# Causal latent attention on pairs of heads, and the order of divisions and maxima in the dilated attention

## What is computed

```python
# latent branch: 8 heads, queries and keys of 64 + 32 features, values of 64, fully causal
s = (einsum('nqhe,nkhe->nhqk', qn_b, k_nope) + einsum('nqhr,nkr->nhqk', qp_b, kpe)) * scale
p, _ = masked_softmax(s, kpos[None, :] <= qpos[:, None])
o = einsum('nhqk,nkhe->nqhe', p, v)
# dilated branch: 8 heads of 64, patterns (window, dilation) = (128, 1), (512, 4), (2048, 16),
# each a banded softmax over strided keys; results combined by their softmax denominators
```

## Time and profile before

| | us |
|---|---|
| median of three runs (lowest, highest) | 2237.77 (2235.47, 2243.18) |
| the profiled execution's own time | 2240.37 |
| its span in the trace | 2238.7 |
| latent prompt attention, from its first to its last work | 555.3 to 736.6 |
| latent sample attention | 736.9 to 875.4 |
| dilated prompt attention, transposes of queries and keys included | 875.7 to 1024.5 |
| PE busy (share of the span) | 2136.0 (95%) |

### The profile page before, as it was taken

How to read it: one execution, slowest core, us unless ns; L and a number is a source line. 1 busy time by engine, 2 the same in 40 slices (tenths; PEclk the granted TensorE clock), 3 DMA queues, 4 the chain that set the end, 5 groups by cost and what they waited for, 6 DMA issues and landing times. The chain is left out here.

```text
span 2238.7 us, 34845 instructions
## 1 busy us (share of the span) xinstructions
PE 2136.0 (95%) x13121; PEld 1810.9 (81%) x13121; DVE 844.9 (38%) x1953; ACT 477.6 (21%) x1036; POOL 723.1 (32%) x483
## 2 busy tenths in 40 slices
PE   7899999999999898888989999999999999999898
PEld 7877799954777334664359999999999999999898
DVE  4244011152767334464324553212211221245575
ACT  5131111131545222452101221100100100112222
POOL 4223043200000220001006665634643653666431
PEclk9999999999999899698999999999999999999999
DMA  6333555200322343205545211111111111111201
GB/s 209 94 111 128 177 199 199 103 20 3 113 95 95 93 135 87 65 2 153 181 142 146 78 47 38 46 49 38 47 47 47 48 47 47 44 43 46 76 29 78
DMA packets 179832, 192.73 MB, mean 86 GB/s; under 512 B 11398, under 2 KB 152582, under 8 KB 178950
## 3 DMA queue, kind: packets, MB, share of 16 engines
q1 hardware_dynamic: 162854, 162.01, 22.8%
q10 hardware_dynamic: 14816, 28.12, 3.6%
q0 software_dynamic: 2048, 1.05, 0.3%
HBM read 160.74 MB, written 63.97 MB: 100 GB/s over the span
## 5 line engine op out<-in xcount | busy, mean ns | idle before, releaser
L638 PE MATMUL bank<-h_hi,wu_hi_tail 128*128 128x352 f32 x960 | 312.0, 325 | 3.4 <-POOL wu_lo_tail L1986 3.4
L1984 POOL TENSOR_TENSOR wu_hi_tail<-w_stage_tail,ones 128x1024 fp32r<-128x1024 f32 x88 | 169.5, 1926 | 436.1 <-DMA w_stage_tail<-in_w_ob 213.8
L639 PE MATMUL bank<-h_lo,wu_hi_tail 128*128 128x352 f32 x960 | 309.4, 322 | 0.0
L640 PE MATMUL bank<-h_hi,wu_lo_tail 128*128 128x352 f32 x960 | 309.2, 322 | 0.0
L638 PE MATMUL bank<-a_hi,wu_hi_tail 128*128 128x352 f32 x768 | 247.7, 323 | 0.0
L639 PE MATMUL bank<-a_lo,wu_hi_tail 128*128 128x352 f32 x768 | 246.1, 320 | 0.0
L640 PE MATMUL bank<-a_hi,wu_lo_tail 128*128 128x352 f32 x768 | 245.9, 320 | 0.0
L1986 POOL TENSOR_TENSOR wu_lo_tail<-w_stage_tail,wu_hi_tail 128x1024 fp32r<-128x1024 f32 x88 | 219.8, 2497 | 6.9
L638 PEld LDWEIGHTS bank<-h_hi,wu_hi_tail 128*128 128x128 f32 x960 | 181.6, 189 | 3.7 <-issue 3.7
L639 PEld LDWEIGHTS bank<-h_lo,wu_hi_tail 128*128 128x128 f32 x960 | 181.7, 189 | 0.0
L640 PEld LDWEIGHTS bank<-h_hi,wu_lo_tail 128*128 128x128 f32 x960 | 181.5, 189 | 0.0
(11 more groups left out here) (288 smaller groups left out, 4096.3 us busy)
## 6 DMA issues: line engine op xcount, KB each, us to landing
w_stage_tail<-in_w_up SPq DMA_DIRECT2D x32, 512.0 KB, 3.9
w_stage_tail<-in_w_down SPq DMA_DIRECT2D x32, 512.0 KB, 3.6
gate_d<-gate_out ACTq DMA_DIRECT2D x16, 528.0 KB, 2.7
f_gates<-gate_d ACTq DMA_DIRECT2D x24, 352.0 KB, 3.1
w_stage_gates<-in_w_in SPq DMA_DIRECT2D x16, 512.0 KB, 3.8
ls_keys<-in_cache_ckv SPq DMA_DIRECT2D x64, 128.0 KB, 2.1
ws_keys<-in_cache_win_k SPq DMA_DIRECT2D x8, 1024.0 KB, 8.4
ws_vals<-in_cache_win_v SPq DMA_DIRECT2D x8, 1024.0 KB, 6.1
```

Of the source, the lines that this page charges most:

```text
L638: pe.matmul(out, w, a, start=n == 0, stop=False)
L639: pe.matmul(out, w, b, start=False, stop=False)
L640: last = pe.matmul(out, v, a, start=False, stop=n == len(ks) - 1)
L1984: pool.tensor_tensor(g.wu_hi[:, j], g.w_stage[:, j], one, ALU.mult).then_inc(g.w_hi, 1)
```

## The change

`attend_latent` replaces `attend_prompt`. It has 32 steps of a pair of heads and a query block. Per side there are two score banks (0 and 1, 2 and 3) and three places of probabilities in place of four for one head at a time; PE runs one step ahead in the scores in place of three, and DVE and ACT work one step ahead in the maxima and exponentials in place of two. The groups of a step (four when i is 4 or more, otherwise two) still alternate between banks 4 and 5. `latent_prob_t` moves to the part of `o_hi` that the dilated branch fills later. `values` alternates between the sides, and `take` handles both in one 128x128 piece. ACT copies all of side 0's groups before the next exponential of side 0, and side 1's before that of side 1. SP's cache copies follow every fourth step. In `attend_window` both divisions of a step stand ahead of both maxima. The core of the diff:

```diff
+    prob = room("latent_prob", [P, 2, 3, SEQ])
+    top = room("latent_top", [P, 2, 3, 4])
+    prob_t = Room(nc, R1, R1 + H // 2 * T * BYTES)("latent_prob_t", [P, 2, 2, NT - 1, P])
-    steps = [(h, i) for h in range(H) for i in reversed(range(NT - 1))]
+    steps = [(pair, i) for pair in range(H // 2) for i in reversed(range(NT - 1))]
...
+        for side in range(2):
+            for j in range(0, i + 1, 4):
+                mine.append((n, side, j, min(j + 4, i + 1)))
+                n += 1
...
             def scores(s):
+                pair, i = steps[s]
+                for side in range(2):
+                    h = 2 * pair + side
+                    if s >= 1:
+                        pe.wait_ge(s_got, 2 * s - 1 + side)
+                    for at in range(0, (i + 1) * P, 512):
+                        w = min(512, (i + 1) * P - at)
+                        last = pe.matmul(g.bank[:, 2 * side + at // 512, :w], q_t[:, h, i * P:(i + 1) * P],
+                                         k_t[:, h, at:at + w], start=True, stop=True)
+                    last.then_inc(s_full, 1)
 
             def transposes(s):
-                pe.wait_ge(p_ready, s + 1)
-                for n, a, b in groups[s]:
+                for n, side, a, b in groups[s]:
+                    pe.wait_ge(p_ready, 2 * s + side + 1)
                     if n >= 2:
                         pe.wait_ge(t_got, n - 1)
...
             def values(s):
...
-                for n, a, b in groups[s]:
-                    pe.wait_ge(t_got, n + 1)
-                    for j in range(a, b):
+                pe.wait_ge(t_got, groups[s][-1][0] + 1)
+                for j in range(i + 1):
+                    for side in range(2):
+                        lo, h = E * side, 2 * pair + side
                         last = pe.matmul(g.bank[lo:lo + E, 6 + s % 2, :P], v[:, j, h * E:(h + 1) * E],
-                                         prob_t[:, s % 2, j, :], start=j == 0, stop=j == i)
+                                         prob_t[:, s % 2, side, j, :], start=j == 0, stop=j == i)
                 last.then_inc(o_full, 1)
...
-            for s in range(3):
-                scores(s)
+            scores(0)
             for s in range(N):
-                if s + 3 < N:
-                    scores(s + 3)
+                if s + 1 < N:
+                    scores(s + 1)
                 transposes(s)
                 if s >= 1:
                     values(s - 1)
...
             def take(s):
...
-                place = (slice(lo, lo + E), tile, slice(i * P, (i + 1) * P))
+                place = (slice(None), H // 2 + pair, slice(i * P, (i + 1) * P))
...
             for s in range(N):
-                divide(s)
-                if s + 2 < N:
-                    largest(s + 2)
+                for side in range(2):
+                    divide(s, side)
+                    if s + 1 < N:
+                        largest(s + 1, side)
                 if s >= 2:
                     take(s - 2)
...
             for s in range(N):
                 if s >= 2:
                     act.wait_ge(o_full, s - 1)
-                for n, a, b in groups[s]:
+                for n, side, a, b in groups[s]:
+                    if side == 1 and a == 0 and s + 1 < N:
+                        exponent(s + 1, 0)
                     act.wait_ge(t_full, n + 1)
...
-                if s + 2 < N:
-                    exponent(s + 2)
+                if s + 1 < N:
+                    exponent(s + 1, 1)
...
@@ attend_window, DVE @@
             for s in range(N):
                 for side in range(2):
                     divide(s, side)
-                    if s + 2 < N:
-                        largest(s + 2, side)
+                for side in range(2 if s + 2 < N else 0):
+                    largest(s + 2, side)
```

More of the change, by code:

```diff
@@ L216, in build @@
             ahead = Ahead(g, kind)
[L217 to L220, removed]
+            (attend_window if kind == "window" else attend_latent)(g, ahead)
             attend_sample(g, kind, ahead)
@@ L984, in _ @@
         def _(sp):
[L985 to L989, removed]
             ahead.load(g, sp)
[L991 to L994, removed]
+            for s in range(NSEQ):
+                sp.wait_ge(o_got, s * (N // NSEQ) + 1)
+                copy_cache(sp, g, g.cache_win_v, g.win_v_sample, s, 1)
         @block.gpsimd
         def _(pool):
-            if not window:
-                ahead.load_rotary(g, pool)
+            ahead.load_rotary(g, pool)
         @block.tensor
@@ L1052, in _, with largest @@
         def _(dve):
-            def largest(s):
-                h, i = steps[s]
+            def largest(s, side):
+                pair, i = steps[s]
                 w = (i + 1) * P
[L1057 to L1061, removed]
+                dve.wait_ge(s_full, 2 * s + side + 1)
+                if s >= 3:
+                    dve.wait_ge(t_full, groups[s - 3][-1][0] + 1)
+                dve.tensor_tensor_reduce(out=prob[:, side, s % 3, :w],
+                                         in0=g.bank[:, 2 * side:2 * side + 2, :].rearrange("p a b -> p (a b)")[:, :w],
@@ L1068, in divide @@
                 w = (i + 1) * P
[L1069 to L1072, removed]
+                dve.wait_ge(e_done, 2 * s + side + 1)
+                dve.reciprocal(top[:, side, s % 3, 3:4], top[:, side, s % 3, 2:3]).then_inc(inv_done, 1)
@@ L1074, in take @@
+                dve.wait_ge(inv_done, 2 * s + side + 1)
+                dve.tensor_scalar(prob[:, side, s % 3, :w], prob[:, side, s % 3, :w], top[:, side, s % 3, 3:4], None,
+                                  ALU.mult).then_inc(p_ready, 1)
             def take(s):
-                h, i = steps[s]
-                lo = E * (h % 2)
-                tile = h // 2 + (0 if window else H // 2)
-                place = (slice(lo, lo + E), tile, slice(i * P, (i + 1) * P))
+                pair, i = steps[s]
@@ L1101, in _, with exponent @@
         def _(act):
-            def exponent(s):
-                h, i = steps[s]
+            def exponent(s, side):
+                pair, i = steps[s]
                 w = (i + 1) * P
[L1105 to L1112, removed]
+                act.wait_ge(s_got, 2 * s + side + 1)
+                act.activation(prob[:, side, s % 3, :w], prob[:, side, s % 3, :w], ACT.Exp, scale=-1.0,
+                               bias=top[:, side, s % 3, 0:1], accum_out=top[:, side, s % 3, 2:3]).then_inc(e_done, 1)
+            exponent(0, 0)
+            exponent(0, 1)
             for s in range(N):
```

69 lines of the change are left out of this document (18 added, 51 removed).

## The result

The changed kernel takes 2183.74 us, the median of four runs (2180.91 to 2187.04); the kernel before, run beside it, 2237.18 (2235.47 to 2243.18). The ratio is 0.9757, with an interval of 0.9734 to 0.978: 53.4 us faster. The forecast was 2195 (2178 to 2213), so the time lies in the range, but two stages missed in opposite directions and the misses cancelled in part.

What follows compares the result with a forecast made beforehand. PE was taken to bound the latent stage, and a ring of waits to slow the dilated stage at full clock. 2240.4 - 29 (latent) - 15 (dilated) = 2196, or 2194 from the median; forecast 2195 us, range 2178 to 2213.

Steps and rivals of the forecast that it cites:

- Part 1: Latent stage: alternating sides takes 576 value passes from 0.107 to 0.053 us each, a gain of 31 us.
- Part 2: Latent stage: 32 steps instead of 64 save 11 us of changing product kinds; PE's work is 33.5 us a pair.
- Part 3: Latent stage: new waits for ACT's copies (wide steps) and side 1's division (narrow steps), each 0.19 to 0.68 us.
- the walk: Latent stage: iteration-by-iteration account of a pair with its waits, 37.1 us a pair, 148.5 for four.
- ACT's order: Latent stage: copies ahead of exponentials free the bank early; ACT, needing 4.8 of 5.7 us at i = 7, isn't the bound.
- DMA: Sample stage: late cache copies charged nothing; without the cover there, at most one copy, 6.4 us.
- Part 4: Dilated stage: divisions first open a ring of waits; a pair takes 24.2 us, the stage about 15 less, bounds 3 and 24.
- comes back at once: Dilated stage rival: the clock doesn't fall or recovers at once, about 14 us more gained, 2181; 9%.
- The moved wait: Dilated stage rival: DVE's new order moves the wait, so the stage gives only 3 us, 2207; 14%.
- the serial chain: Latent stage rival: one step of lookahead doesn't cover the chain, 47 us a pair, stage 190, kernel 2248; 3%.
- The rule of no overlap: Latent stage rival: weight loads don't overlap, values cost 0.107 each, the stage gains about 4 us, 2221; 4%.
- Half clock to the end of the stage: Dilated stage rival: the clock stays at half, a pair takes 43 us, 2.6 pairs lose 49, kernel 2244; 4%.

Runs made afterwards that it cites:

- e3: Changed kernel with all value products of side 0 ahead of those of side 1 in the latent stage, no alternation; 2202.36 us.
- e4: Changed kernel with PE doing the previous step's values between the two sides' transposes in the latent stage; 2164.27 us.
- e5: Changed kernel with ACT's exponential of a side ahead of that side's copies in the latent stage; 2187.43 us.
- e1: Changed kernel with the old order of divisions and maxima put back in the dilated stage, so the latent part alone; 2212.44 us.
- e11: Changed kernel run again unaltered, as a measure of the spread; 2181.88 us.
- e8: Changed kernel with the old dilated order, and the next stage's load held back until the dilated stage's values have landed; 2201.63 us.
- e2: Kernel before with only the new order, both divisions ahead of both maxima, in the dilated stage; 2206.17 us.

## Why the prediction was right or wrong

**Part 1 (alternating sides, 31 us): right.** The loads are 0.051 apart, as read from the dilated stage, against 0.105 before, and 576 passes times the difference are 31 us. e3's 19 doesn't speak against it, since its sides still meet once in each step.

**Part 2 (half as many steps, PE's own work 33.5 a pair): right.** e4, with the waits gone, shows 34.12.

**Part 3 (new waits): right in place, undersized.** The waits are where they were put: the third group waits for ACT's copy in wide steps and side 1's division delays narrow ones. The iterations from i = 7 to 0 took 5.97, 6.91, 6.16, 5.39, 4.00, 3.26, 2.52 and 4.55, where the walk had 5.7, 6.5, 5.7, 5.0, 3.9, 3.2, 2.5 and 4.6. The narrow ones are right to 0.1. The wide ones are short by 0.3 to 0.5 each, 1.53 of the 1.66 a pair that are missing. The step that failed is "0.43 (first group) + 0.1 + 0.6 = 1.13 after the start": it is 1.44 in each iteration shown. At i = 4 to 6 that adds 0.31, less up to 0.07 where the fourth group no longer waits. At i = 7 it adds 0.31 - 0.18 + 0.03, since the walk's wait of 0.18 before the fourth group goes and the values start 0.03 late. The scores add another 0.1 each: from 599.70 to 602.81 they take 3.11 us for 28 passes, 3.00 by 0.107. Together that is 1.4 of 1.53. Times four pairs the 1.66 is 6.6 us, which covers the miss of the stage (158.6 against 152.4; by its own terms, 148.5 + 5.9 - 3.4 + 1.2, the forecast comes to 152.2).

**ACT's order: as said.** ACT isn't the bound. That copies stand ahead of exponentials is worth 2.6 us (e5).

**DMA (nothing for the cache copies): right.** The sample stage took 137.9 against 138.8, and no wait for its pages came in its first part.

**Part 4 (dilated stage, 15 us): right in direction, half the size.** The 29 measured lie above even the bound of 24 that was set for all waits going. Two steps of the sum failed.
- "Two steps in eight hold a take ... 4.0, longer than PE. So a pair takes ... 24.2." It takes 22.79, with PE busy in 22.41. The operations of a take and PE's next transposes in the changed kernel:

```profile
906.83 1.13 DVE L1255 CAST o_hi<-bank 128x512 fp32r<-128x512 f32 x1
907.99 1.10 DVE L1257 TENSOR_TENSOR o_lo<-bank,o_hi 128x512 fp32r<-128x512 f32 x1
```

```profile
909.66 0.31 PEld L1185 LDWEIGHTS bank<-ident,window_prob 128*128 128x128 f32 x3 [0.42 <-DVE window_prob L1246]
...
910.19 0.31 PEld L1185 LDWEIGHTS bank<-ident,window_prob 128*128 128x128 f32 x3 [0.22 <-DVE window_prob L1246]
```

  DVE is two steps ahead in the maxima, and PE waits 0.42 and 0.22 us for the two divisions behind the take, 0.6 in all, where the sum had 4.0 - 2.7 = 1.3. Twice in a pair, that is the 1.4 between 24.2 and 22.8. So a mean of DVE's time over a few steps (18.73/8 = 2.3 us, less than PE's 2.7) would have been nearer than that of one step. (That no transposes would wait over 0.3 was wrong too; the longest wait, 1.3, stands at the last step of the stage.)
- "In the slow part PE is the bound and some 3 are left" and "2.6 pairs" at full clock. In the changed kernel half clock ended 7 us after the first value products and not 43. What this is worth can be told from the times between the first value products and the stage's end: before 124.3, e1 116.5, e11 93.6, changed 90.7. Before and e1 have the same code there and 41.0 and 17.1 us at half clock: 8 us for the clock. e1 and e11 have the same 17.1 and differ in the order: 23 for the order, of which some 2 may be e1's further fall at its end (before has it, e8 hasn't, and with the same 41.0 they take 124.3 and 122.6). e11 and changed are one program with 17.1 and 10.2: 3 more for the clock. The changed kernel's value products start 4.6 later after their long DMA wait. 8 + 23 + 3 - 5 is the 29 measured. The prediction charged nothing to that wait; e11, with 1.2 us of it, shows that the change doesn't always bring it.

**Rivals.** The clock that "comes back at once" had 9% and came true in part: it fell in every run, and came back after 7 to 17 us in nine of the ten with the new order. It had been worked out at 14 us; for the difference between before and e1 it is 8. The moved wait and the serial chain didn't happen: the pairs of 22.79 and 38.76 speak against them. The rule of no overlap did not hold. Half clock to the end of the stage occurred in no run.

**The net.** The gain was put 6 too high in the latent stage and 14 too low in the dilated one, and the sample stage gave 0.9: 8.9 in all between the profiled runs. By the medians 2195 is 11 above 2183.7. Either miss alone would have left the time in the range too; that it came within 11 of the forecast and not 15 is luck.

## What to carry to other kernels

Products with 64 columns of weights should alternate between the halves of the array, block by block: it halved their price here (0.105 to 0.051 us). Where transposes go through a small ring of banks, put PE's independent work (here the previous step's values) between the groups, since the path PE to ACT to PE cost 0.4 us here beside the copy itself, and order the divisions that need only old results ahead of maxima that wait for PE. When a ring of waits is opened, ask how far ahead the other engines run before a long operation is charged to a single step.

## What the runs showed of the hardware

- Value loads of the 128x64 form that alternate between the sides start 0.051 us apart over full 128 rows, and 0.105 on one side; run one side after the other, 32 loads average 0.095, and behind the first two only six distances, where the sides meet, are under 0.06 (e3).
- A copy by ACT began 0.27 us after the fourth transpose should have ended, and PE took 0.14 to go on after the copy, in three iterations of three.
- The granted clock falls to half in the dilated stage near the first value products in every run, and stays there for 7 to 41 us, with PE busy in over 90% of it in e8 (39.8 of 43 us at 0.52). The length differs between profiles of one program (10.2 and 17.1). The runs of one kernel differ too, which may be the same thing: e1's six runs differ by 17 us, e2's by 1.4.
